# Turning the differential keys by VectorE squares and DRAM instead of by TensorE, with VectorE's order rewritten around the scores

## What is computed

```python
h = rms_norm(x, pre_w, NORM_EPS)
proj = jnp.einsum('bsd,dn->bsn', h, w_in)
dq, dk, dv, dg, sq, sk, sv, sg, iq, ik, iw = jnp.split(proj, SPLIT_OFFSETS, axis=-1)
dq = apply_rope(dq.reshape(b, s, 4, 2, 64), cos_d, sin_d)
dk = apply_rope(dk.reshape(b, s, 4, 2, 64), cos_d, sin_d)
oa = diff_attention(dq, dk, dv, lam)      # softmax of two maps per head, p0 - lam * p1, times dv
oa = rms_norm(oa, subln_w, SUBLN_EPS) * (1.0 - lambda_init) * jax.nn.silu(dg)
ob = dsa_attention(sq, sk, sv, iq, ik, iw)   # per query the 64 keys with the highest indexer score
ob = ob * jax.nn.silu(sg)
y = jnp.einsum('bsm,md->bsd', jnp.concatenate([oa, ob], -1), w_out)
return x + rms_norm(y, post_w, NORM_EPS)
```

## Time and profile before

| | |
|---|---|
| median of 3 runs (lowest, highest) | 302.94 us (302.40, 303.06) |
| the profiled execution's own time | 302.85 us |
| its span | 301.1 us |
| VectorE busy | 78% of the span |
| ACT busy | 54% |
| GpSimd busy | 22% |
| TensorE's mean granted clock | 0.996 |

### The profile page before, as it was taken

One profiled execution on the slowest core, in us unless ns is written; L12 is line 12 of the kernel. 1 busy time (PEld: TensorE's weight loads), 2 busy tenths in 40 slices (PEclk: granted clock), 3 DMA queues, 4 the chain that ended last, 5 costly groups with the idle time before them and its releaser, 6 DMA issues.

```text
span 301.1 us, 4401 instructions
## 1 busy us (share of the span) xinstructions
PE 292.4 (97%) x1568; PEld 246.4 (82%) x1568; DVE 234.9 (78%) x474; ACT 163.9 (54%) x284; POOL 67.6 (22%) x116
## 2 busy tenths in 40 slices
PE   8999999999999999999999999999999999999992
PEld 7799777788787888788888988778878788887892
DVE  4752989899999997955984786878999999787343
ACT  5986963736577473603665855473737747390101
POOL 6558210303030220101060740012303030210101
PEclk9999999999999999999999999999999999999998
DMA  7999959457518569860059799937653675742011
GB/s 242 370 371 386 371 214 354 135 143 227 195 69 210 209 211 303 191 201 23 0 158 369 242 350 250 325 108 204 209 150 131 146 272 152 202 70 72 0 70 70
DMA packets 62229, 60.01 MB, mean 199 GB/s; under 512 B 34560, under 2 KB 39424, under 8 KB 62208
## 3 DMA queue, kind: packets, MB, share of 16 engines
q1 hardware_dynamic: 61920, 59.47, 62.8%
q10 hardware_dynamic: 288, 0.26, 0.3%
HBM read 54.48 MB, written 5.24 MB: 198 GB/s over the span
## 4 chain that ended last, share of the span: by engine, by line
PE 40%; DVE 37%; ACT 8%; DMA 6%; POOL 4%; issue 3%; SPq 1%; POOLq 0%; DVEq 0%; ACTq 0%
DVE w_lo L987 14%; PE bank_a L470 8%; PE bank_a L461 7%; PE bank_a L466 7%; PE bank_s L618 6%; DMA w_raw<-in_w_in 6%; PE bank_a L618 5%; ACT xt_pbuf L831 4%; DVE work L1107 4%; DVE xt_pbuf L1124 3%; DVE top L1106 3%; DVE xt_pbuf L1140 3%; DVE mixn L1150 2%; DVE mixn L1036 2%; PE bank_s L559 1%
## 5 line engine op out<-in xcount | busy, mean ns | idle before, releaser
L987 DVE TENSOR_TENSOR w_lo<-w_raw,w_hi 128x2048 fp32r<-128x2048 f32 (+1 forms) x46 | 98.8, 2154 | 18.5 <-ACT w_hi L763 18.3
L763 ACT ACTIVATE w_hi<-w_raw 128x2048 fp32r<-128x2048 f32 (+1 forms) x46 | 81.9, 1784 | 31.9 <-PE bank_a L470 23.4
L461 PE MATMUL bank_a<-w_hi,h_hi 128*128 128x512 f32 (+1 forms) x272 | 72.5, 388 | 0.0
L470 PE MATMUL bank_a<-w_lo,h_hi 128*128 128x512 f32 (+1 forms) x272 | 70.0, 379 | 0.5 <-DVE w_lo L987 0.5
L466 PE MATMUL bank_a<-w_hi,h_lo 128*128 128x512 f32 (+1 forms) x272 | 69.9, 379 | 0.0
L470 PEld LDWEIGHTS bank_a<-w_lo,h_hi 128*128 128x128 f32 x272 | 49.7, 188 | 10.5 <-DVE w_lo L987 1.0
L466 PEld LDWEIGHTS bank_a<-w_hi,h_lo 128*128 128x128 f32 x272 | 49.8, 188 | 9.8
L461 PEld LDWEIGHTS bank_a<-w_hi,h_hi 128*128 128x128 f32 x272 | 47.9, 188 | 10.4 <-issue 2.7
L831 ACT ACTIVATE xt_pbuf<-xt_pbuf,st 128x128 f32<-128x128 f32 (+1 forms) x48 | 21.3, 444 | 25.1 <-DVE st L1124 25.1
L1417 POOL TENSOR_TENSOR rt<-nat,tab 128x256 f32<-128x256 f32 x10 | 7.4, 741 | 112.5 <-ACT nat L815 112.5
L815 ACT ACTIVATE nat<-bank_a,st 128x512 f32<-128x512 f32 x20 | 13.5, 681 | 19.6 <-PE bank_a L470 19.6
(11 more groups left out here) (196 smaller groups left out, 431.1 us busy)
## 6 DMA issues: line engine op xcount, KB each, us to landing
w_raw<-in_w_in SPq DMA_DIRECT2D x30, 1024.0 KB, 6.0
w_raw<-in_w_out SPq DMA_DIRECT2D x8, 1024.0 KB, 6.1
w_raw<-in_w_in SPq DMA_DIRECT2D x8, 584.0 KB, 7.3
turned<-mixn SPq DMA_DIRECT2D x20, 128.0 KB, 2.7
prm<-in_rows SPq DMA_DIRECT2D x2, 705.0 KB, 7.0
w_raw<-in_w_in SPq DMA_DIRECT2D x2, 512.0 KB, 6.3
xres<-in_x SPq DMA_DIRECT2D x2, 512.0 KB, 9.5
dqT<-turned SPq DMA_DIRECT2D x2, 512.0 KB, 5.9
```

The source lines that it names most:

```text
L461: pe.matmul(bank, h_hi[:, HALF * half + kk, tok], whi[:, kk, :], start=half == 0 and kk == 0, stop=False)
L470: mm = pe.matmul(bank, h_hi[:, HALF * half + kk, tok], wlo[:, kk, :], start=False, stop=half == 1 and kk == HALF - 1)
L763: act.activation(unit(w_hi, u), unit(raw, u), ACT.Copy).then_inc(hi_done.sem, 1)
L987: dve.tensor_tensor(unit(w_lo, u), unit(raw, u), unit(w_hi, u).bitcast(F32), ALU.subtract).then_inc(lo_done.sem, 1)
```

## The change

The keys of the differential mixer take the second way as well. VectorE turns squares of dk (`turn_squares(0, 3, ...)`) behind the mask of block 0, SP puts them to a new DRAM tensor and gets them into `dkT` in two DMAs, one per block; TensorE's `turn_nat(T_DK, ...)` and VectorE's `drain_pair(T_DK, dkT)` are gone. The first scores move from behind `first(13)` to behind `first(14)`, two chunk halves later, and the pieces after them move too. ACT waits for the squares of dk before it writes sk to the same buffer, and moves group 15 before the exponentials of use 10. VectorE's list between the choice and the first gate is in another order, and in the output phase `gate_dsa(0)` goes ahead of `drain_mix(T_MD1)`. Line numbers are 7 (TensorE) to 9 (VectorE, ACT) higher after the change.

```diff
# SP, in the loop over u
                     if u == 14:
                         sp.wait_ge(dq_put.sem, dq_put.at(layer, 16 * SQUARES))
                         get(1, dqT, dq_landed.sem)
+                    if u == 14:
+                        sp.wait_ge(dk_squares.sem, dk_squares.at(layer, 1))
+                        put(DKS, squares, dk_put.sem)
+                        sp.wait_ge(dk_put.sem, dk_put.at(layer, 16 * SQUARES))
+                        for b in range(BLOCKS):
+                            sp.dma_start(dkT[:, :, b * P:(b + 1) * P], scratch[DKS][:, b * HEADS:(b + 1) * HEADS, :]).then_inc(dk_landed.sem, 16)
# TensorE
                 second(12)
-                turn_nat(T_DK, 0, 3)
                 first(13)
-                pe.wait_ge(t_drained.sem, t_drained.at(layer, T_DK + 2))
+                second(13)
+                first(14)
                 pe.wait_ge(dq_landed.sem, dq_landed.at(layer, dq_landed.per_layer))
+                pe.wait_ge(dk_landed.sem, dk_landed.at(layer, dk_landed.per_layer))
                 diff_scores(6, 0, range(HEADS))
                 diff_scores(8, 1, (0, 1))
-                second(13)
-                first(14)
                 second(14)
                 first(15)
+                diff_scores(10, 1, (2, 3))
+                second(15)
+                first(16)
                 pe.wait_ge(combined.sem, combined.at(layer, 1))
                 turn_probs(T_PD0, 6, 0, HEADS)
-                diff_scores(10, 1, (2, 3))
-                second(15)
                 pe.wait_ge(combined.sem, combined.at(layer, 2))
                 turn_probs(T_PD1A, 8, 1, 2)
-                first(16)
                 second(16)
                 turn_nat(T_SK, 0, 5)
                 first(17)
-                pe.wait_ge(combined.sem, combined.at(layer, 3))
-                turn_probs(T_PD1B, 10, 1, 2)
                 pe.wait_ge(t_drained.sem, t_drained.at(layer, T_SK + 2))
                 pe.wait_ge(sq_landed.sem, sq_landed.at(layer, sq_landed.per_layer))
                 dsa_scores(12, 0, range(HEADS))
+                pe.wait_ge(combined.sem, combined.at(layer, 3))
+                turn_probs(T_PD1B, 10, 1, 2)
# ACT
+                    if chunk == SK:
+                        act.wait_ge(dk_squares.sem, dk_squares.at(layer, 1))
...
                 split_hi(layer, 18)
+                move(15)
                 exps(10, 1, 2)
                 exps(11, 1, 2)
-                move(15)
# VectorE
                 mask_unchosen(0)
+                dve.wait_ge(dq_put.sem, dq_put.at(layer, 16 * SQUARES))
+                turn_squares(0, 3, dk_squares.sem)
                 split_lo(layer, 14)
-                choose(1, 1)
-                drain_pair(T_DK, dkT)
+                choose(1, 3)
+                split_lo(layer, 15)
                 choose(1, 2)
-                split_lo(layer, 15)
                 mask_scores(6, 0, 4, causal[:, P:SEQ])
                 mask_scores(7, 0, 4, causal[:, P:SEQ])
-                choose(1, 2)
+                split_lo(layer, 16)
+                mask_scores(8, 1, 2, causal[:, :])
+                mask_scores(9, 1, 2, causal[:, :])
...
                 combine(6, 0, HEADS, 0)
-                mask_scores(8, 1, 2, causal[:, :])
-                mask_scores(9, 1, 2, causal[:, :])
-                dve.wait_ge(dq_put.sem, dq_put.at(layer, 16 * SQUARES))
+                dve.wait_ge(dk_put.sem, dk_put.at(layer, 16 * SQUARES))
                 turn_squares(1, 4, sq_squares.sem)
-                split_lo(layer, 16)
                 combine(8, 1, 2, 0)
+                split_lo(layer, 17)
                 drain(T_PD0, pT[:, 0, :])
                 mask_scores(10, 1, 2, causal[:, :])
                 mask_scores(11, 1, 2, causal[:, :])
-                split_lo(layer, 17)
+                drain(T_PD1A, pT[:, 1, :])
+                choose(1, 1)
+                drain_pair(T_SK, skT)
+                combine(10, 1, 2, 2)
+                split_lo(layer, 18)
+                mask_scores(12, 0, 4, work[0][:, :])
+                drain(T_PD1B, pT[:, 2, :])
                 choose(1, 2)
-                drain(T_PD1A, pT[:, 1, :])
-                combine(10, 1, 2, 2)
-                choose(1, 1)
                 mask_unchosen(1)
-                drain_pair(T_SK, skT)
-                split_lo(layer, 18)
-                drain(T_PD1B, pT[:, 2, :])
-                mask_scores(12, 0, 4, work[0][:, :])
+                turn_probs(PS0, 12)
                 split_lo(layer, 19)
-                turn_probs(PS0, 12)
                 split_lo(layer, 20)
...
                 gate_diff(1)
                 split_lo(layer, 22)
+                gate_dsa(0)
                 drain_mix(T_MD1, m_hi, m_lo, 1, subln)
-                gate_dsa(0)
                 drain_mix(T_MS0, h_hi, h_lo, 0)
```

More of the change, by code:

```diff
@@ L86 @@
 ROW_N = sum(ROW.values())
[L89 to L92, removed]
+T_IK, T_PD0, T_PD1A, T_SK, T_PD1B = 4, 5, 6, 7, 9
+T_MD0, T_MD1, T_MS0, T_MS1 = 10, 11, 12, 13
+T_USES = 14
+DKS, PS0, PS1 = range(3, 6)
 LANES = 32
@@ L235, in build_trunk @@
         iq_squares, iq_landed = sem("iq_squares"), sem("iq_landed")
+        dk_squares, dk_put, dk_landed = count("dk_squares", 1), count("dk_put", 16 * SQUARES), count("dk_landed", 16 * BLOCKS)
         dq_squares, sq_squares = count("dq_squares", 1), count("sq_squares", 1)
```

## The result

The changed kernel takes **305.95 us** (median of 4 runs, 305.25 to 306.58) against 302.86 for the kernel before (4 runs, 302.40 to 303.06): a ratio of 1.0101, with an interval of 1.0088 to 1.0114. It is slower by 3.1 us. The forecast was 303.2 with a range of 302.2 to 304.9; the result lies above it. The profiled execution took 305.88, 3.03 above that of before, and its span is 304.1.

What follows compares the result with a forecast made beforehand. TensorE, busy 292.4 of 301.1 us, was taken as the bound. Per layer -0.88 + 1.13 + 0.52 - 0.70 read as +0.07, plus 0.1 for the keys' DMAs: 0.17, twice 0.35, on 302.85 gives 303.2 us, range 302.2 to 304.9.

Steps and rivals of the forecast that it cites:

- Removed from TensorE, -0.88: TensorE's eight transposes of the keys go, saving 0.88 us per layer in full.
- The new wait at first(15), 1.13: TensorE waits 1.13 us per layer at first(15) for ACT's move of group 13, which shares the bank.
- the rival without this wait: ACT's move comes in time, so TensorE does not wait at first(15): 300.9 us, chance 0.06.
- The keys in time: At the first scores, the keys' gets land near 81.22 with TensorE there at 81.19; scores start 0.1 us late.
- The first rival: Keys' gets land late at the first scores, up to 1.73 us per layer: 304.7 to 306.4 us, chance 0.26.
- the near end: The keys' gets take 3.6 us, as 512 KB with nothing ahead in the queue, rather than 5.3.
- The third mix turn's wait gone, -0.70: With the gate ahead of the drain, TensorE's 0.70 us wait per layer for VectorE at the third mix turn goes.
- The second mix turn, 0.52: TensorE waits 0.52 us more per layer at the second mix turn, as VectorE's gates end at 124.34.
- VectorE has time at the drain of the first probabilities: VectorE stands at the drain of the first probabilities at 96.22, 1.17 us before their bank is full.
- The fourth rival: GpSimd's rotation slows the low part ahead of the first probabilities' drain, shifting 0.5 us per layer: 304.2 us, chance 0.06.

Runs made afterwards that it cites:

- experiment 6: Changed kernel with squares back between low parts 19 and 20, ACT's group 13 move ahead of the exponentials, one choice round ahead of the first masks: 300.47 us.
- experiment 4: Kernel before the change, with only gate_dsa(0) put ahead of drain_mix(T_MD1): 301.85 us, 0.9960 of the kernel before.
- experiment 2: Changed kernel with ACT's move of group 13 ahead of the exponentials of uses 6 and 7: 303.64 us, 1.0016 of the kernel before.
- experiment 3: Changed kernel with gate_dsa(0) back behind drain_mix(T_MD1): 308.60 us, 1.0180 of the kernel before.
- experiment 1: Changed kernel with VectorE's squares of the first probabilities back between low parts 19 and 20: 304.39 us, 1.0040 of the kernel before.
- experiment 7: Changed kernel with two choice rounds and the block 1 mask between low parts 19 and 20, squares ahead of them: 306.42 us, 1.0118.

## Why the prediction was wrong, point by point

- **Removed from TensorE, -0.88: right.** The transposes are gone; experiment 6 against experiment 4 gives 0.87, net of what moved with them.
- **The new wait at first(15), 1.13: right, and 0.12 short.** It was 1.25, with ACT's move as releaser, and it goes when the move stands ahead of the exponentials (experiment 2). So the rival without this wait did not occur.
- **The keys in time: right.** The put of the keys started at 72.71 (72.54 in the forecast) and the gets at 77.50 (77.62); the scores started 81.47 - (80.39 + 0.91) = 0.17 behind the half before them. The rows of SP's queue, and of the DMA issues (how many, KB each, us to landing):

```profile
72.71 2.76 SPq L320 DMA_DIRECT2D turned<-mixn  x4
77.50 0.92 SPq L375 DMA_DIRECT2D dkT<-turned  x2
```

```profile
dkT<-turned SPq DMA_DIRECT2D x4, 256.0 KB, 3.3
```

  The first rival, the keys landing late, which had 0.26, did not occur. By the Trainium skill (DMA: Bandwidth & Descriptors, section Specifications) pieces of 512 B move at line rate. The 3.3 us for each get agree with the near end that the prediction took (3.6); no run here moves these bytes in smaller pieces.
- **The third mix turn's wait gone, -0.70: right.** No wait at 129.96; 0.75 comes back when the gate goes behind the drain (experiment 3), and 1.1 us in all is gained by the gate alone (experiment 4).
- **The second mix turn, 0.52: this failed.** It was 1.56. The step is "The new one has the same instructions between drain and first gate, less one low part [...], so the gate starts at 114.48". It counted VectorE's instructions from the drain to the gate and took the gate to start when VectorE gets there. VectorE got there at 110.52 + 4.45 = 114.97, 0.49 behind the forecast; then it stood 0.92 for GpSimd's root. The row that told of this was among those read: in the earlier trace rows the first gate of the kernel before has [1.21 <-POOL st L1404]. The prediction subtracted those 1.21 to find VectorE's end and did not ask when the root would be done in the new order. Of the 1.04 that this term is too small by, 0.92 is the wait on GpSimd, and experiment 1 takes back 1.01 by moving the squares alone. There the second mix turn is 0.56 late: the count of VectorE's own list was right, and the wait on GpSimd was missing from it.
- **VectorE has time at the drain of the first probabilities: right.** It waited 1.95 there, against 1.17 in the forecast. The fourth rival, a low part ahead of that drain slowed by GpSimd, did not occur.

The fourth rival had the right pair of engines and the wrong direction. The prediction looked for a low part slowed by a rotation, with the Trainium skill's rule that GpSimd shares SBUF interfaces with VectorE instructions of two SBUF inputs (GPSIMD Engine Reference, section 1 Specifications). What cost time is the reverse: the low part goes on at its usual pace, two in 4.45, and the small GpSimd step stands. The Trainium skill, SBUF — State Buffer, section SBUF: two separate sides, puts it more sharply: the shared ports are a lock, held for a whole instruction by the engine that came first (VectorE with two SBUF inputs, or GpSimd), while the other is fully blocked. The trace agrees for the addition, which ended 0.07 after the low part that was running when it came, in the changed kernel and 0.06 after it in experiment 7. The other way round the traces show both. In the kernel before, a low part that began at 70.51, 0.10 into the last step of a rotation (70.41 to 71.15), took 2.79 (in layer 1 too, at 215.13), where an undisturbed one takes 2.25 to 2.29:

```profile
70.51 2.79 DVE L987 TENSOR_TENSOR w_lo<-w_raw,w_hi 128x2048 fp32r<-128x2048 f32 x1
```

But in experiment 1 a low part began at 112.19 beside the power (111.79 to 112.82) and took its usual 2.25, and so it was in experiment 6; for the power the rule does not hold as far as these spans tell, and spans on POOL are rough.

Per layer the forecast had +0.17 and the trace has +1.41. Of the 1.24 between them 1.04 is the second mix turn, 0.12 the wait at `first(15)`, and 0.08 is spread over the rest.

## What to carry to other kernels

Where an engine waits for a tiny step of another one, that step has a schedule of its own: before moving work, ask what runs beside it in the new order, above all where a GpSimd step that somebody waits for would begin inside a long VectorE instruction like the low parts here. A gap of under a microsecond between two such instructions, filled with other work, was worth 1.6 us here, without an instruction more. And when a step moves in one engine's list, look in the lists of the engines that follow it: here ACT's unchanged order held a ready move behind exponentials that came later, and one line there was worth 2.3 us.

## What was not expected of the hardware

A GpSimd addition over 128x4 numbers took 0.20 us beside VectorE's squares and 1.51 when it began in a low part; the power behind it took 1.01 and 2.94. How long such a step takes depends on the end of VectorE's instruction, not on its own size: the addition began 0.81 into a low part in the changed kernel and took 1.51, began 1.89 into one in experiment 7 and took 0.42, and began beside the squares in experiment 6 and took 0.20. A step that had begun was not held: the power took 1.03 with a low part starting 0.40 into it in experiment 1, and 0.14 into it in experiment 6.
